# Expert look-ups of a two-block transformer kernel: who splits the weights there, how the candidates are added, and the order of spills and of the last chunk

## The reference

```python
q = (xt @ w_query).reshape(T, PEER_HEADS, 2, QUERY_HALF)
s = jnp.einsum('thpd,hpnd->thpn', q, sub_keys)
s_top, i_top = lax.top_k(s, PEER_TOPK)
cand = s_top[:, :, 0, :, None] + s_top[:, :, 1, None, :]       # 16 x 16 sums per head
cand_idx = i_top[:, :, 0, :, None] * N_KEYS + i_top[:, :, 1, None, :]
g_s, sel = lax.top_k(cand, PEER_TOPK)
idx = jnp.take_along_axis(cand_idx, sel, axis=-1)
g = jax.nn.softmax(g_s, axis=-1)
# per token, over the 8 heads x 16 chosen experts
a = jnp.einsum('td,thkd->thk', xc, expert_u[idx])
y = jnp.einsum('thk,thkd->td', g * gelu(a), expert_v[idx])
```

## Time and profile before

| | us |
|---|---|
| median of three runs | 2914.46 |
| the profiled execution, whole | 2911.84 |
| its span | 2910.0 |
| TensorE busy | 2798.0 (96%) |
| VectorE busy | 2330.1 (80%) |
| ScalarE busy | 1382.2 (47%) |
| GpSimd busy | 655.7 (23%) |
| all w_lo by VectorE for other sets (L2125), 400 | 874.3 |
| w_lo by GpSimd (L3026), 60 | 253.4 |

### The profile page before, as it was taken

How to read it: one execution, slowest core, us unless ns; L and a number is a source line. 1 busy time by engine, 2 the same in 40 slices (tenths; PEclk the granted TensorE clock), 3 DMA queues, 4 the chain that set the end, 5 groups by cost and what they waited for, 6 DMA issues and landing times.

```text
span 2910.0 us, 48733 instructions
## 1 busy us (share of the span) xinstructions
PE 2798.0 (96%) x19360; PEld 2600.3 (89%) x19360; DVE 2330.1 (80%) x3480; ACT 1382.2 (47%) x1553; POOL 655.7 (23%) x435
## 2 busy tenths in 40 slices
PE   5999899999999999999999999999999999999999
PEld 3888788888889888789999999999999999999998
DVE  7888768888875775667999978888777989968787
ACT  4444544454444444454445554444444345555443
POOL 2310313113131120004451113221005441012221
PEclk9999999999999999999999999999999999999999
DMA  7787237777843465334457779999454567779997
GB/s 295 286 279 264 85 144 263 283 256 278 286 161 116 167 219 178 118 111 166 174 188 257 257 263 330 369 368 381 163 194 168 173 218 250 258 284 337 350 400 288
DMA packets 161910, 700.13 MB, mean 241 GB/s; under 512 B 15240, under 2 KB 61488, under 8 KB 105536
## 3 DMA queue, kind: packets, MB, share of 16 engines
q1 hardware_dynamic: 122720, 559.65, 53.4%
q10 hardware_dynamic: 20576, 70.85, 6.6%
q0 software_dynamic: 18432, 67.12, 6.3%
HBM read 667.07 MB, written 30.42 MB: 240 GB/s over the span
## 4 chain that ended last, share of the span: by engine, by line
PE 52%; DVE 10%; DMA 3%; issue 1%; ACT 1%; SPq 0%; ACTq 0%; DVEq 0%
PE pp L1371 7%; PE pp L1437 6%; PE mz L1437 6%; PE pp L631 5%; PE pp L1373 3%; PE mz L1439 3%; PE pp L1439 3%; DMA raw<-expert_v 3%; PE pp L633 3%; PE pp L642 2%; PE pp L644 2%; PE pp L643 2%; PE mz L1426 2%; PE pp L1349 1%; PE pp L1351 1%
## 5 line engine op out<-in xcount | busy, mean ns | idle before, releaser
L2125 DVE TENSOR_TENSOR w_lo<-raw,w_hi 128x2048 fp32r<-128x2048 f32 (+1 forms) x400 | 874.3, 2186 | 266.9 <-ACT w_hi L1545 265.6
L1545 ACT ACTIVATE w_hi<-raw 128x2048 fp32r<-128x2048 f32 (+1 forms) x486 | 893.4, 1840 | 391.9 <-DMA raw<-expert_v 192.7
L631 PE MATMUL pp<-hs,w_hi 128*128 128x512 f32 x1408 | 510.9, 405 | 23.4 <-POOL hs L3114 13.3
L3026 POOL TENSOR_TENSOR w_lo<-raw,w_hi 128x2048 fp32r<-128x2048 f32 (+1 forms) x60 | 253.4, 4238 | 868.0 <-ACT w_hi L1545 867.8
L633 PE MATMUL pp<-hs,w_lo 128*128 128x256 f32 x1408 | 399.5, 284 | 0.0
L1437 PE MATMUL mz<-w_split,w_hi 128*128 128x448 f32 x1024 | 354.2, 377 | 6.7 <-DVE w_lo L2125 6.7
L1437 PE MATMUL pp<-w_split,w_hi 128*128 128x448 f32 x1024 | 353.5, 376 | 4.7 <-DVE w_split L2853 4.5
L631 PEld LDWEIGHTS pp<-hs,w_hi 128*128 128x128 f32 x1408 | 269.3, 191 | 96.9 <-DVE w_lo L2125 9.8
L631 PE MATMUL pp<-us,w_hi 128*128 128x512 f32 x960 | 345.1, 403 | 8.8 <-DVE both L2153 4.2
L1371 PE MATMUL pp<-hs,w_hi 128*128 128x448 f32 x1024 | 328.7, 377 | 0.0
L1349 PE MATMUL pp<-hs,w_hi 128*128 128x224 f32 x1024 | 284.8, 278 | 12.7 <-DVE w_lo L2139 12.7
(11 more groups left out here) (363 smaller groups left out, 5735.4 us busy)
## 6 DMA issues: line engine op xcount, KB each, us to landing
raw<-expert_u SPq DMA_DIRECT2D x128, 1024.0 KB, 4.9
raw<-expert_v SPq DMA_DIRECT2D x128, 1024.0 KB, 7.2
raw<-ffn_in SPq DMA_DIRECT2D x88, 1024.0 KB, 4.9
ada_raw<-ada ACTq DMA_DIRECT2D x116, 512.0 KB, 5.2
raw<-ffn_down SPq DMA_DIRECT2D x64, 704.0 KB, 4.5
raw<-out_w SPq DMA_DIRECT2D x16, 1024.0 KB, 4.8
raw<-hgrn SPq DMA_DIRECT2D x16, 1024.0 KB, 4.8
raw<-query SPq DMA_DIRECT2D x16, 1024.0 KB, 4.8
```

Source lines behind the costliest of these rows:

```text
L631: mm(outp, w_hi[:, slot, a:a + P], rhs[:, k0 + k].rearrange("p a t -> p (a t)"), start=(k0 + k == 0), stop=False, skip_group_check=True)
L1545: f(w_hi[:, slot, 0:n], raw[:, slot, 0:n], ACT.Copy).then_inc(hi_ready, 1)
L2125: v.tensor_tensor(w_lo[:, slot, 0:n], raw[:, slot, 0:n], w_hi[:, slot, 0:n].bitcast(F32), ALU.subtract)\
```

## The change

Four things change.

1. `DVE_SPLITS`: VectorE now makes `w_lo` of (8, 0) and (15, 1), and no longer of (13, 0), which GpSimd makes. In the first block's look-ups there are five splits and one behind the ids; (7, 1) moves from behind the ids to ahead of the second reduction. In the second block's there are four, and (15, 1) behind the gates' subtraction.
2. `candidates`: the 16 x 16 sums are made per head, by a scalar_tensor_tensor of 128 x 256, right before that head's search.
3. SP: the spill of a second-set chunk stands behind the weight transfer of its own j, where both spills stood behind both transfers.
4. The last chunk of the second set: `high(0)` on ScalarE and `low(0)` on VectorE, which make the first `w_split`, stand ahead of the split of the next weights.

```diff
-DVE_SPLITS = ((5, 1), (6, 0), (6, 1), (7, 0), (7, 1), (13, 0), (13, 1), (14, 0), (14, 1), (15, 0))
+DVE_SPLITS = ((5, 1), (6, 0), (6, 1), (7, 0), (7, 1), (8, 0), (13, 1), (14, 0), (14, 1), (15, 0),
+              (15, 1))
...
-            def weights(ph, after=None):
+            def weights(ph, after=None, behind=None):
...
                         sp.dma_start(raw[:, 2 * half + j, 0:n], src[bass.ds(2 * rp + j, 1)]).then_inc(landed[2 * half + j], 16)
+                        if behind:
+                            behind(j)
...
-            def spill(l, rp):
-
-                for j in range(2):
-                    sp.wait_ge(gelu_done, HALF_CHUNKS * (2 * l + 1) + 2 * rp + j + 1)
-                    sp.dma_start(act_dram[2 * rp + j], act_out[:, j]).then_inc(act_spilled[j], 16)
-                if rp % 2 == 0 and rp > LEAD:
+            def spill(l, rp, j):
+
+                sp.wait_ge(gelu_done, HALF_CHUNKS * (2 * l + 1) + 2 * rp + j + 1)
+                sp.dma_start(act_dram[2 * rp + j], act_out[:, j]).then_inc(act_spilled[j], 16)
+                if j and rp % 2 == 0 and rp > LEAD:
...
-                        weights(ph.part(rp, 1))
-                        if rp > 1:
-                            spill(l, rp - 2)
+                        weights(ph.part(rp, 1), behind=(lambda j: spill(l, rp - 2, j)) if rp > 1 else None)
...
                             gelu_joined(n - 1)
+                        if n == HALF_CHUNKS - 1:
+                            act.wait_ge(gate_spilled[1], unit_count(l + 1, 1))
+                            act.wait_ge(g_used, STEPS * (l + 1))
+                            high(0)
                         split_next(ph, rp, pair, half, lap, j)
...
-                        if n == HALF_CHUNKS - 1:
-                            act.wait_ge(gate_spilled[1], unit_count(l + 1, 1))
-                            act.wait_ge(g_used, STEPS * (l + 1))
-                            high(0)
...
-                    a_ = tv[:, :, 0].unsqueeze(3).to_broadcast([P, 4, TOPK, TOPK])
-                    b_ = tv[:, :, 1].unsqueeze(2).to_broadcast([P, 4, TOPK, TOPK])
-                    link(v.tensor_tensor(cand.rearrange("p h (a b) -> p h a b", b=TOPK), a_, b_, ALU.add))
                     for h in range(4):
+                        a_ = tv[:, h, 0].unsqueeze(2).to_broadcast([P, TOPK, TOPK])
+                        b_ = tv[:, h, 1].unsqueeze(1).to_broadcast([P, TOPK, TOPK])
+                        link(v.scalar_tensor_tensor(cand[:, h].rearrange("p (a b) -> p a b", b=TOPK), a_, 1.0, b_, ALU.mult, ALU.add))
                         top16(best_v[:, tb, h0 + h], best_i[:, tb, h0 + h], cand[:, h])
...
                         link(v.tensor_tensor(e, e, tf[:, :, s].unsqueeze(2).to_broadcast(wide), ALU.mult))
+                        if s and not tb:
+                            split_here(l, 4)
                         link(v.tensor_reduce(ij_f[:, s, tb].rearrange("p (h k) -> p h k", k=TOPK), e, AX.X, ALU.add))
...
-                        split_here(l, 4)
+                        split_here(l, 5)
...
-                split_here(l, 9)
+                split_here(l, 10)
...
+                        if n == HALF_CHUNKS - 1:
+                            dve.wait_ge(g_used, STEPS * (l + 1))
+                            low(0)
                         if rp + 1 not in POOL_HALVES:
                             split_next(ph, rp, pair, half, j)
...
-                dve.wait_ge(g_used, STEPS * (l + 1))
-                low(0)
                 join(HALF_CHUNKS - 1)
```

More of the change, by code:

```diff
@@ L555, in _ @@
                     for rp in range(ph.pairs):
-                        weights(ph.part(rp, 1))
-                        if rp > 1:
-                            spill(l, rp - 2)
+                        weights(ph.part(rp, 1), behind=(lambda j: spill(l, rp - 2, j)) if rp > 1 else None)
                 elif ph.kind == "expert_v" and ph.index % 2 == 0:
                     for rp in range(2):
-                        weights(ph.part(rp, 1))
-                        spill(l, ph.pairs - 2 + rp)
+                        weights(ph.part(rp, 1), behind=lambda j: spill(l, ph.pairs - 2 + rp, j))
                     weights(ph.part(2, 10))
@@ L2707, in candidates @@
                     tv = top_v[:, tb, 2 * h0:2 * h0 + 8].rearrange("p (h s) k -> p h s k", s=2)
[L2708 to L2710 removed]
                     for h in range(4):
+                        a_ = tv[:, h, 0].unsqueeze(2).to_broadcast([P, TOPK, TOPK])
+                        b_ = tv[:, h, 1].unsqueeze(1).to_broadcast([P, TOPK, TOPK])
+                        link(v.scalar_tensor_tensor(cand[:, h].rearrange("p (a b) -> p a b", b=TOPK), a_, 1.0, b_, ALU.mult, ALU.add))
                         top16(best_v[:, tb, h0 + h], best_i[:, tb, h0 + h], cand[:, h])
                 def look_up(l, tb):
[L2716 removed]
+                    split_here(l, 6 * tb)
                     v.tensor_copy(top_b[:, tb], top_i[:, tb])
@@ L2726, in look_up @@
                                              iota_b[:].unsqueeze(1).unsqueeze(1).to_broadcast(wide), ALU.is_equal))
-                        split_here(l, 5 * tb + 1 + 2 * s)
+                        split_here(l, 6 * tb + 1 + 2 * s)
                         link(v.tensor_tensor(e, e, tf[:, :, s].unsqueeze(2).to_broadcast(wide), ALU.mult))
+                        if s and not tb:
+                            split_here(l, 4)
                         link(v.tensor_reduce(ij_f[:, s, tb].rearrange("p (h k) -> p h k", k=TOPK), e, AX.X, ALU.add))
                         if s == 0:
-                            split_here(l, 5 * tb + 2)
+                            split_here(l, 6 * tb + 2)
                 dve.wait_ge(key_mm, TB * l + TB)
@@ L2815, in join @@
                     v.tensor_tensor(act_out[:, n % 2], act_out[:, n % 2], pp[:, 1 - n % 2, :, 0:TD], ALU.add).then_inc(sum_done, 1)
-                take_routes()
-                dve.wait_ge(lo_ready, 2 * ph.pair0 + 2)
-                for rp, pair, half, lap in each_pair(ph):
-                    for j in range(2):
-                        n = 2 * rp + j
-                        if n:
-                            join(n - 1)
-                        if n == LEAD + 1:
-                            dve.wait_ge(gelu_done, HALF_CHUNKS * (2 * l + 1))
-                        if 0 <= n - LEAD - 1 < STEPS:
-                            times(n - LEAD - 1, (n - LEAD - 1) % 2)
-                        if 0 <= n - LEAD + 1 < STEPS:
-                            build(n - LEAD + 1, (n - LEAD + 1) % 2)
-                        if rp + 1 not in POOL_HALVES:
-                            split_next(ph, rp, pair, half, j)
-                        elif j == 0:
-                            split_even(pair + 1, 1 - half)
                 def weigh(n):
@@ L2853, in low @@
                     v.tensor_tensor(w_split[:, m % 2, :, 1], src, w_split[:, m % 2, :, 0].bitcast(F32), ALU.subtract).then_inc(ws_lo, 1)
-                dve.wait_ge(g_used, STEPS * (l + 1))
-                low(0)
+                take_routes()
+                dve.wait_ge(lo_ready, 2 * ph.pair0 + 2)
+                for rp, pair, half, lap in each_pair(ph):
+                    for j in range(2):
+                        n = 2 * rp + j
+                        if n:
+                            join(n - 1)
+                        if n == LEAD + 1:
+                            dve.wait_ge(gelu_done, HALF_CHUNKS * (2 * l + 1))
+                        if 0 <= n - LEAD - 1 < STEPS:
+                            times(n - LEAD - 1, (n - LEAD - 1) % 2)
+                        if 0 <= n - LEAD + 1 < STEPS:
+                            build(n - LEAD + 1, (n - LEAD + 1) % 2)
+                        if n == HALF_CHUNKS - 1:
+                            dve.wait_ge(g_used, STEPS * (l + 1))
+                            low(0)
+                        if rp + 1 not in POOL_HALVES:
+                            split_next(ph, rp, pair, half, j)
+                        elif j == 0:
+                            split_even(pair + 1, 1 - half)
                 join(HALF_CHUNKS - 1)
```

## The result

Timed against the kernel before, eleven runs each, the changed kernel took 2920.26 us in the median (2917.97 to 2931.61), the one before 2906.54 (2893.59 to 2922.83): a ratio of 1.0044, 95% interval 1.0027 to 1.0062. It is slower by 12.8 us, where I had forecast 1.5 us less. That 2920.26 still lies in the range that I gave (2893 to 2926) is partly luck: I counted from 2914.46, the median of three runs of before, and eleven have 2906.54. The profiled executions show only half of the difference: 2917.97 against 2911.84, +6.1. The profile of before happened to spend 6.5 us more ahead of the first expert set, in parts that the change does not touch: its first GELU there is at 1348.43, the one after at 1341.92.

The account below looks back on a forecast made before the run. TensorE, busy for 96% of the span, bounds the kernel, so only its pauses and the slow clock behind them count. First sets +8.5 us and V products -10.0 sum to -1.5; forecast 2912 us, range 2893 to 2926.

Parts of the forecast that it names:

- the walk: First set: per-head additions wait for GpSimd's splits, giving TensorE pauses of 8.1 us before chunk 11, 2.2 before chunk 27.
- The old pauses before chunks 15 and 30: First set: pauses and their clock go, 12.0 us in the first layer, 6.9 in the second (chunk 15 only).
- The V starts: Where the V products begin: the last chunk's new order gains 5.0 us per layer, 10.0 together.
- the spills: Second set: SP's new order frees chunk 30's copy earlier but by itself gains nothing.
- (8, 0) and (7, 1): First block's look-ups: both splits done in time, (7, 1) at about 1429 when TensorE wants it at 1434.
- the slower rival: Second set's start: TensorE waits up to 4.6 us for w_lo plus 1.9 for the clock, twice; 2925, chance 0.15.
- these come about 1.0 late: Ahead of chunk 31: split (15, 1) and the normalised gates about 1.0 us late, bounds 0 and 5.6.
- The price of the clock: Slow clock behind a TensorE pause of over 3 us: 1.9 us, other end 2.75; nothing behind one of 2 us.
- the 0.5 of the look-up: Second token block: a look-up with four splits takes 21.9 us against 21.4 for four chunks, adding 0.5.
- my first rival: Candidates: per-head additions don't wait for GpSimd, or hardly; 28.9 us go, 2885, chance 0.12.

Follow-up runs that it names:

- e5: The kernel before with the order of the spills alone changed; V starts of 200.05 and 200.04 us, 2.9 and 3.1 shorter.
- e6: The kernel before with the order of the last chunk alone changed; V starts of 198.82 and 198.66 us.
- e1: The changed kernel with the candidates added for four heads at once again; 2881.84 us, ratio 0.9897 to the kernel before.
- e2: The kernel before with the spills and the last chunk alone changed; ratio 0.9971 to the kernel before.
- e8: The changed kernel with split (15, 1) moved behind the product that normalises the gates; ratio 1.0011 to the kernel before.
- e4: The changed kernel with each head's addition as a tensor_tensor instead of a scalar_tensor_tensor; first sets of 190.25 and 190.67 us.
- e7: The kernel before with the new share and order of the splits alone; ratio 0.9950 to the kernel before.
- e11: The kernel before with only split (7, 1) moved ahead of the second reduction; first sets of 175.58 and 176.07 us.
- e3: The kernel before with the candidates per head alone changed; ratio 1.0041 to the kernel before.

## Why the prediction was wrong

**Right.** TensorE's pauses decide. VectorE's two-input operations wait for GpSimd's split and step with it: pauses of 8.15 and 2.12 us where the walk gave 8.1 and 2.2. The old pauses before chunks 15 and 30 went. The V starts gave 10.4 for the 10.0 forecast, with shares that I had not seen: I put the spills at nothing, and alone they give 2.9 and 3.1 us (e5); with the spills late I had all in time still, and TensorE waits 0.3 us (e6). (8, 0) and (7, 1) were in time. The second set's first chunks did not wait for `w_lo`: the V start, which contains that set, is 197.90 in the change and in e1 and e2 alike, so the slower rival's place was not hit, though its sum, 2925, was nearer than my 2912.

**The step that failed** is "these come about 1.0 late (estimate; bounds 0, and 5.6 with a GpSimd split in front of the gate product)". It was 6.30 and 6.47, above its upper bound: 5.3 + 5.5 of the miss of 14.8 on the first sets of both layers. I took the value near the bound of nothing, though the mechanism that I had just read from the earlier trace rows said the reverse: `gate_n` has two SBUF inputs, and GpSimd's two splits for the next pair are let loose when ScalarE writes that pair's `w_hi` at chunk 31's door, which is when the gates are late. e8 takes 6.28 and 6.45 off by moving one instruction past the other. The price of the clock behind that pause (6.30 less 3.76 = 2.5 us) was missing from the bound too.

**The second error is behind chunks 11 and 27.** Behind the pause before chunk 11 the clock cost 2.42 and 2.73 (10.57 and 10.88 less 8.15), where I took the low end, 1.9: 1.4 together. Chunk 27 cost 4.0 in each layer where I had 2.7 with the 0.5 of the look-up: 2.6 over both. I took nothing for the clock there, and it did fall. Length, busy PE, PEld, DVE, ACT, POOL (count), clock, DMA share, GB/s, from the end of the pause before chunk 11, and 2 us behind the end of the one before chunk 27:

```profile
1403.60:1405.60 2.00, 1.97 (x9) 1.97 (x10) 1.93 (x5) 0.00 (x0) 0.00 (x0) 0.50 0.00 0
...
1497.70:1499.70 2.00, 2.00 (x12) 2.00 (x11) 1.97 (x2) 0.00 (x0) 0.00 (x0) 0.50 0.06 21
```

But e4 had the same pause without the fall and lost as much by chunk 31 (10.5 and 10.6 us against 10.3 and 10.5). As these two kernels show it, VectorE sets the pace from chunk 27 on: its splits and then the gates end when they end, and a TensorE that is faster waits longer for them. So the terms of this stretch, 2.2 + 0.5 + 1.0 = 3.7 per layer, were too small as a whole, and the clock behind chunk 27's pause is not what made them so.

With the gates' 10.8 and 1.4 from chunk 11, chunk 27's 2.6 makes 14.8; 1.2 went the other way, since before's steps of chunks 11 to 13 (5.46, 5.47 and 5.76) are even now. The sum of first sets, forecast +8.5, is +22.1, and +22.1 - 10.4 = +11.7. A miss of some 14 us is 0.5%, all of it from small terms at the low end of their bounds: with the upper ends that the text itself names for the gates (5.6) and the clock (2 x 0.85 + 2 x 1.9) the sum would have been -1.5 + 9.2 + 5.5 = +13.2. Two slips of arithmetic in the prediction are smaller than that: 1424.0 less four chunks and 0.3 is 1402.3 and not 1402.1, and 2912 with 2 x 0.85 + 2 x 1.9 is 2917.5 and not 2919.

**What the change was worth.** Splits: -18.9 us of first set (e7). Spills and last chunk: -10.4 (e2). Additions per head on top of these: +41.0 of first set (after less e1). With four heads in one addition the kernel takes 2881.84 us.

## What to carry to other kernels

An instruction that has to wait for a shared resource pays once for each time it is issued, so in a stretch where another engine holds it most of the time (4.6 of every 5.4 us here), one large operation is cheaper than four small ones of the same work (19.1 us for e1's eight, 55.2 for the change's 32). Where an operation is known to collide and its partner is let loose by the same event that makes it urgent, take the colliding end of the bound, or put the small urgent one first. Removing one pause often moves it to the next late instruction (e11), and adding one often hides another (e3): measure a change of parts by each of them on a kernel where the others are already in time.

## What the runs showed of the hardware

The same pause did and did not bring the clock down. In the first layer of e8 TensorE stood for 2.11 us at the same place as in the change, and kept full clock:

```profile
1501.37 0.37 PE L1348 MATMUL pp<-hs,w_hi 128*128 128x224 f32 x1 [2.11 <-DVE w_lo L2138]
```

```profile
1503.00:1505.00 2.00, 2.00 (x20) 2.00 (x20) 1.97 (x2) 0.00 (x0) 0.00 (x0) 1.00 0.22 86
```

In the change the same stretch ran 12 matmuls at 0.50 (1.2 GHz in place of 2.4). The loss differed little all the same. In e8 the steps of chunks 27 to 30 are 3.8 us above the even ones (7.73, 5.46, 5.78 and 6.31), since TensorE at full clock came to VectorE's splits before they were done (waits of 0.17 before chunk 29 and 0.66 before chunk 31). In the change it came later and found them done, and chunk 27 alone is 4.0 above. What decides whether the clock falls stays open.

The rule in the Trainium skill that bounded my first rival, "Advanced Engine Details and Errata", section VectorE Performance Modes, names only VectorE's two-port modes as what GpSimd blocks; the additions of e4 with two float32 tensors took 2.80 us beside a split and 0.42 without one, so that rule, read as the whole of it, does not hold here. The Trainium skill's "SBUF — State Buffer", section "SBUF: two separate sides", has the operations with two SBUF inputs as well, against a GpSimd operation that reads SBUF, and the rows shown here agree with it.
